# One pass of 512 columns for the high weights in the MLP's down projections, modulation rows and attention bias spread over the MLP, first softmax groups normalised by GpSimd

## The chip, the core and the metric

One core of a Trainium2 chip runs the whole program as one launch. The metric is the time of an execution in device microseconds (us). Two of the executions of the kernel before are within 0.1% of each other, and the third is 0.5% above them.

## What is computed

The program takes 256 tokens of width 1024 through three layers: a recurrent layer with an MLP, a sparse attention layer with an MLP, and a hybrid layer of neighbourhood attention and two convolution branches. The change touches the MLPs, the softmax of the attention layer, and the modulation rows of the third layer:

```python
def sq_relu_mlp(h, w_up, w_down):
    return jnp.square(jax.nn.relu(h @ w_up)) @ w_down

    for layer in range(DEPTH):
        ...
        x = x + mix
        x = x + sq_relu_mlp(rms_norm(x, norm_mlp_g[layer]), mlp_w_up[layer], mlp_w_down[layer])

    # attention layer, per block of 128 queries
        p = jax.nn.softmax(logits, axis=-1).astype(c.dtype)

def modulate(x, cond, norm_g, w_ada, b_ada):
    shift, scale, gate = jnp.split(jax.nn.silu(cond) @ w_ada + b_ada, 3, axis=-1)
    ...
    return rms_norm_2(x, norm_g) * (1 + scale) + shift, gate
```

`w_up` is 1024 x 4096 and `w_down` 4096 x 1024. `modulate` is taken of the tokens with `c_2` and of the context with `c_ctx_2`; the gate rows are wanted for the tokens alone.

## The kernel before

Activations lie transposed: a tile is 128 features by 256 tokens. Every matrix is cut into chunks of 128 x 1024 numbers (512 KB), eight 128 x 128 blocks each. 266 chunks pass through a ring of four slots: SyncE's queue loads `raw`, ScalarE copies it to the reduced type (`whi`, the high part), VectorE subtracts (`wlo`, the low part), and TensorE multiplies. SyncE loads the next chunk into a slot as soon as VectorE has made `wlo` of the old one. The activations are split in the same way. The function `acc3` makes one product tile from three passes into one accumulator: high weights by high activations (L546), high weights by low activations (L550), low weights by high activations (L551). Each pass loads its 128 x 128 weights and streams 256 columns.

An MLP has two stages. In the first (`up0`, `up1`: 16 units of two chunks) VectorE takes the relu, ScalarE squares it twice into `hhi` and `sqb`, and VectorE makes `hlo`. In the second (`down0`, `down1`: 16 units) two units, that is four chunks or 32 blocks, make one output tile m of eight: 96 passes into the first 256 columns of bank 0 or 1, in turn. VectorE adds the bank to `x[:, m]` (L1696), ScalarE makes `xh` of it, VectorE `xl`, and the next stage (`lat` after `down0`, the context's keys `ck` after `down1`) multiplies by these; it can begin with its tiles k = 0 to 6 and needs k = 7 last. Between the first and the second half of `down0` a full-precision product with `ones` (L598) sums the context's squares. In the unit after it the table PACE cuts six of the first passes in two (L548, L549). The same table is used in one unit each of `up0`, `up1` and `gates`.

The modulation needs 24 row tiles of `w_ada`, 512 KB each, loaded by GpSimd's queue into two slots (`load_ada`), each reduced against `cond` by VectorE: twice for shift and scale tiles, once for the 8 gate tiles. Eight tiles (two reduces each) lie beside `up0` (`ada_beside`, L1631), sixteen (24 reduces) beside `down0` (`ada_tile`, L1558), two per m. The loads of the attention bias `relB`, 8 of 256 KB, are issued one per m in `down0` behind GpSimd's addition of squares.

The attention layer's softmax runs in 12 groups. Per group TensorE makes logits (L799, L804), VectorE adds the bias and takes the maximum (`read_logits`, L1803), ScalarE takes the exponential and its sums, VectorE inverts the sums and scales `pt` (`norm_probs`, L1813), TensorE transposes (L813) and multiplies by V (L825). Groups 0 to 3 have four pieces of 128 x 128, the others two of 128 x 256. The last four of the eight rounds of the top-k search and the scaling of the last queries (`queries(3)`, L1773) stand between these groups on VectorE. TensorE's logits of group 3 wait for `queries(3)`.

The order on each engine is the order of the code, written out by hand. `quads` is a loop over groups of four units.

## Time and profile before

| | us |
|---|---|
| three executions | 861.98, 862.42, 866.18 |
| median | 862.42 |
| profiled execution | 861.54 |
| its span, first to last instruction | 859.5 |

| stage | us from the span's start |
|---|---|
| recurrent layer | 0 to 94 |
| `up0`, `down0` | 94 to 184, 184 to 273 |
| `lat`, `q`, search, attention, `att_out` | 273 to 380 |
| `up1`, `down1` | 380 to 468, 468 to 555 |
| third layer | 555 to 859 |

In the rows, PE is TensorE's matmul stream, PEld its weight loads, DVE VectorE, ACT ScalarE, POOL GpSimd, SPq SyncE's queue. A row of the time order has the start, the duration, the engine, the line, the operation, what it writes and reads, the shape and the number of instructions merged, and in brackets the idle time before it and what ended it. A matmul's duration is its passage through the array and overlaps its neighbours': what it costs is the distance from its start to the next one's.

### The profile page before, as it was taken

How to read it: one execution, taken by the hardware profiler on the slowest of the kernel's cores; microseconds unless marked ns; L12 is line 12 of the kernel's file. 1: busy time of each engine (PE TensorE's matmuls, PEld its weight loads, DVE VectorE, ACT ScalarE, POOL GpSimd, SP SyncE). 2: the span in 40 equal slices, each digit the busy share in tenths (PEclk: the TensorE clock that was granted, in tenths of full speed). 3: DMA queues.
4: the chain of work that ended last, by engine and by line, in shares of the span. 5: the costliest groups of instructions: out<-in, count | busy, mean ns of one | idle time of the engine just before them, and what ended most of it. 6: DMA issues, size and time to landing. Idle time of an engine off the chain costs nothing.

```text
span 859.5 us, 18107 instructions
## 1 busy us (share of the span) xinstructions
PE 848.9 (99%) x7062; PEld 813.6 (95%) x7062; DVE 698.2 (81%) x1096; ACT 484.3 (56%) x710; POOL 130.0 (15%) x147
## 2 busy tenths in 40 slices
PE   8999999999999999999999999999999999999998
PEld 7999999999999997799999999989899898999998
DVE  5998798898888899786667666677758998998895
ACT  6796555555444466765555444363367557645742
POOL 3140000014322000000000222132203314012000
PEclk9999999999999999999999999999999999999999
DMA  8744667779999730246666666576445554455552
GB/s 318 299 149 147 221 229 245 244 258 294 296 289 267 216 128 20 93 162 214 196 195 196 203 193 195 167 214 220 149 148 172 171 161 159 148 174 177 207 180 98
DMA packets 48050, 167.88 MB, mean 195 GB/s; under 512 B 5969, under 2 KB 7393, under 8 KB 47729
## 3 DMA queue, kind: packets, MB, share of 16 engines
q1 hardware_dynamic: 41840, 146.82, 52.0%
q0 software_dynamic: 5856, 20.00, 8.0%
q8 instruction: 47, 0.77, 0.4%
q14 instruction: 19, 0.15, 0.1%
q10 hardware_dynamic: 288, 0.15, 0.1%
HBM read 165.50 MB, written 1.44 MB: 194 GB/s over the span
## 4 chain that ended last, share of the span: by engine, by line
PE 74%; DVE 14%; DMA 6%; ACT 3%; issue 2%; SPq 0%; POOL 0%; DVEq 0%; ACTq 0%
PE bank L546 22%; PE bank L550 22%; PE bank L551 22%; DMA raw<-weights 5%; DVE wlo L1416 4%; DVE xc L1498 1%; DVE ada_prod L1558 1%; PE bank L813 1%; ACT whi L1030 1%; PE bank L898 1%; PE bank L900 1%; PE bank L899 1%; PE bank L939 1%; PE bank L949 1%; DMA x<-x_in 1%
## 5 line engine op out<-in xcount | busy, mean ns | idle before, releaser
L1416 DVE TENSOR_TENSOR wlo<-raw,whi 128x1024 fp32r<-128x1024 f32 x266 | 326.8, 1262 | 86.1 <-ACT whi L1030 85.5
L550 PE MATMUL bank<-xl,whi 128*128 128x256 f32 x1328 | 369.7, 278 | 0.0
L546 PE MATMUL bank<-xh,whi 128*128 128x256 f32 x1310 | 367.5, 281 | 1.9 <-DVE xl L1438 1.7
L551 PE MATMUL bank<-xh,wlo 128*128 128x256 f32 x1328 | 368.4, 277 | 0.0
L1030 ACT ACTIVATE whi<-raw 128x1024 fp32r<-128x1024 f32 x266 | 272.3, 1054 | 152.6 <-PE bank L551 99.6
L546 PEld LDWEIGHTS bank<-xh,whi 128*128 128x128 f32 x1310 | 245.8, 188 | 10.9 <-issue 7.1
L550 PEld LDWEIGHTS bank<-xl,whi 128*128 128x128 f32 x1328 | 249.4, 188 | 0.3
L551 PEld LDWEIGHTS bank<-xh,wlo 128*128 128x128 f32 x1328 | 249.2, 188 | 0.0
L551 PE MATMUL bank<-hhi,wlo 128*128 128x256 f32 x560 | 155.1, 277 | 0.0
L546 PE MATMUL bank<-hhi,whi 128*128 128x256 f32 x554 | 154.1, 278 | 0.0
L550 PE MATMUL bank<-hlo,whi 128*128 128x256 f32 x512 | 142.2, 278 | 0.0
L551 PEld LDWEIGHTS bank<-hhi,wlo 128*128 128x128 f32 x560 | 105.2, 188 | 0.0
L546 PEld LDWEIGHTS bank<-hhi,whi 128*128 128x128 f32 x554 | 104.0, 188 | 0.3
L550 PEld LDWEIGHTS bank<-hlo,whi 128*128 128x128 f32 x512 | 96.1, 188 | 0.0
L1175 ACT ACTIVATE hhi<-tq 128x512 f32 (+1 forms) x32 | 20.3, 635 | 73.2 <-DVE tq L1665 73.2
L1965 DVE SCALAR_TENSOR_TENSOR cu<-up,cols,cu 128x256 f32<-128x256 f32 x120 | 49.1, 480 | 0.0
L412 POOL TENSOR_TENSOR acc<-acc,sqt 128x256 f32<-128x256 f32 x16 | 18.7, 1169 | 183.6 <-ACT sqt L1192 183.6
L546 PE MATMUL bank<-hch,whi 128*128 128x256 f32 x160 | 45.6, 285 | 0.4 <-DVE hcl L1821 0.4
L550 PE MATMUL bank<-hcl,whi 128*128 128x256 f32 x160 | 44.6, 279 | 0.0
L551 PE MATMUL bank<-hch,wlo 128*128 128x256 f32 x160 | 44.6, 279 | 0.0
L546 PEld LDWEIGHTS bank<-hch,whi 128*128 128x128 f32 x160 | 30.0, 188 | 1.5 <-issue 0.7
L1558 DVE CUSTOM_DVE_ANT_0 ada_prod<-ada_raw,cond 128x1024 f32<-128x1024 f32 x24 | 29.9, 1245 | 1.4
(311 smaller groups left out, 1032.1 us busy)
## 6 DMA issues: line engine op xcount, KB each, us to landing
raw<-weights SPq DMA_DIRECT2D x266, 512.0 KB, 4.3
ada_raw<-ada_w POOLq DMA_DIRECT2D x24, 512.0 KB, 5.7
plain<-plain_w SPq DMA_DIRECT2D x8, 512.0 KB, 8.5
relB<-rel_scratch POOLq DMA_DIRECT2D x8, 256.0 KB, 8.8
bl<-rpb_in POOLq DMA_DIRECT2D x32, 64.0 KB, 3.4
plain<-plain_w SPq DMA_DIRECT2D x4, 256.0 KB, 5.7
cond<-cond_in POOLq DMA_DIRECT2D x1, 1024.0 KB, 8.5
cx<-ctx_in POOLq DMA_DIRECT2D x1, 1024.0 KB, 8.5
```

The source lines that it names most:

```text
L412: ins = G.tensor_tensor(acc[:, 0], acc[:, 0], sqt[:, 0], ALU.add)
L546: mmul(dst, hi, rh, start=start, stop=False)
L550: mmul(dst, hi, rlo, start=False, stop=False)
L551: return mmul(dst, lo, rh, start=False, stop=stop)
L813: mm = nc.tensor.transpose(TURN[:, i * P:(i + 1) * P], src[:, g % depth, i * P:(i + 1) * P], ident[:])
L898: mmul(dst, rh[:, k, tok], wh, start=k == 0, stop=False)
L899: mmul(dst, rh[:, k, tok], wl, start=False, stop=False)
L1030: A(whi[:, sl], raw[:, sl], ACT.Copy).then_inc(S_["w_hi_ready"], 1)
L1175: A(hhi[:, bass.ds(q * 8 + 2 * (r - u0), 2)], tq[:, r % 2], ACT.Square).then_inc(S_["h_hi"], 1)
L1416: V_.tensor_tensor(wlo[:, sl], raw[:, sl], whi[:, sl].bitcast(F32), ALU.subtract)\
L1558: ins = V_.tensor_tensor_reduce(ada_prod[:], ada_raw[:, slot], cond[:, c], 1.0, 0.0, ALU.mult, ALU.add, dst(c))
L1965: ins = V_.scalar_tensor_tensor(cu[:, t], up[:, t, k:k + S], wk, cu[:, t], ALU.mult, ALU.add)
```

## The change

- In both down stages the block of high weights is multiplied by the high and the low activations in one pass of 512 columns (`h2` holds `hhi` and `hlo` in one tensor); the results lie in the two halves of the bank. The low weights' pass goes into the first half. VectorE adds both halves to `x[:, m]`, one after the other. The cut passes of `down0` go.
- Of the 24 row tiles two gate tiles (one reduce each) go to the stage before `up0`, eight stay in `up0`, fourteen (22 reduces) are left in `down0`, three reduces per m at most and two in m = 4 and m = 7. The order of the tiles is changed to suit.
- All eight `relB` loads are issued in `up0`, one behind each row load.
- `norm_probs` of groups 0 to 3 is done by GpSimd after VectorE has inverted the sums.
- The first plain weights are loaded by halves of a chunk (2 KB per partition in one piece), where it was quarters of two chunks, and their first slot is freed earlier.

```diff
-ADA_ORDER = [0, 1, 2, 3, 4, 5, 6, 7, 8, 16, 9, 17, 10, 18, 11, 19, 12, 20, 13, 21, 14, 22, 15, 23]
+ADA_ORDER = [16, 17, 0, 1, 2, 3, 4, 5, 6, 7, 8, 18, 9, 19, 10, 20, 11, 21, 12, 13, 22, 14, 23, 15]
-ADA_DOWN = 8
+ADA_UP = 2
+ADA_DOWN = ((10, 11), (12, 13), (14, 15), (16, 17), (18,), (19, 20), (21, 22), (23,))
...
-            hhi = sb("hhi", [P, FT, S], F32R, room)
-            hlo = sb("hlo", [P, FT, S], F32R, room)
+            h2 = sb("h2", [P, 2, FT, S], F32R, room)
+            hhi, hlo = h2[:, 0], h2[:, 1]
...
-                sp.dma_start(plain[:, 0:2, part], plain_w[0:2, :, part].rearrange("c p n -> p c n")).then_inc(s_head[j], 16)
+                sp.dma_start(plain[:, j // 2, part], plain_w[j // 2][:, part]).then_inc(s_head[j], 16)
...
+            load_ada(2)
+            load_ada(3)
             pool.wait_ge(S_["chunk_used"], 2 * U0["up0"])
             pool.dma_start(cx[:], ctx_in).then_inc(S_["ctx_loaded"], 16)
-            for i in range(2, ADA_DOWN + 2):
-                load_ada(i)
...
+            pool.wait_ge(S_["rel_stored"], 16)
+            for m in range(DT):
+                load_ada(4 + m)
+                load_rel_bias(m)
             pool.dma_start(wiw[:], wi_in).then_inc(S_["wi_loaded"], 16)
-            pool.wait_ge(S_["rel_stored"], 16)
-            squares_by_tile(3, 0, ahead_of_tile, load_rel_bias)
+            squares_by_tile(3, 0, ahead_of_tile)
...
+            for g in range(4):
+                pool.wait_ge(S_["sums_inverted"], g + 1)
+                for i in range(4):
+                    sl = slice(i * P, (i + 1) * P)
+                    ins = G.tensor_scalar(pt[:, g % 3, sl], pt[:, g % 3, sl], rden[:, g % 2, i:i + 1], None, ALU.mult)
+                ins.then_inc(S_["probs_ready"], 1)
...
-                            mm = acc3(b[:, 0:S], (2 * r + c) % 4, k * P, hhi[:, kt], hlo[:, kt], kt == 0, kt == FT - 1,
-                                      pace.get((c, k)))
+                            sl, w = (2 * r + c) % 4, slice(k * P, (k + 1) * P)
+                            mmul(two(b), whi[:, sl, w], h2[:, :, kt], start=kt == 0, stop=False)
+                            mm = mmul(b[:, 0:S], wlo[:, sl, w], hhi[:, kt], start=False, stop=kt == FT - 1)
...
-                    quads(pe, u0 + 8, u0 + 9, lambda q, r: unit(q, r, PACE))
-                    quads(pe, u0 + 9, u0 + NUNITS["down0"], unit)
+                    quads(pe, u0 + 8, u0 + NUNITS["down0"], unit)
...
                 add_pair(0, j)
+                if j in (1, 2):
+                    ada_tile(j - 1)
...
-                        ada_tile(ADA_DOWN + 2 * m)
-                        ada_tile(ADA_DOWN + 2 * m + 1)
+                        for i in ADA_DOWN[m]:
+                            ada_tile(i)
...
-                    emptied(V_.tensor_tensor(x[:, m], bank[(F0["down" + name] + m) % 2][:, 0:S], x[:, m], ALU.add))
+                    b = bank[(F0["down" + name] + m) % 2]
+                    ch.link(V_.tensor_tensor(x[:, m], b[:, 0:S], x[:, m], ALU.add))
+                    emptied(V_.tensor_tensor(x[:, m], b[:, S:2 * S], x[:, m], ALU.add))
...
-                ch.link(V_.reciprocal(rden[:, g % 2, 0:2 * nt], den[:, g % 2, 0:2 * nt]))
+                ins = V_.reciprocal(rden[:, g % 2, 0:2 * nt], den[:, g % 2, 0:2 * nt])
+                if g < 4:
+                    ins.then_inc(S_["sums_inverted"], 1)
+                    return
+                ch.link(ins)
+                if g == 4:
+                    dve.wait_ge(S_["probs_ready"], 4)
```

TensorE in the middle of `down0`, at the product with `ones`, before the change. L546 and L550 read the same block of `whi`:

```order
L546 MATMUL bank<-hhi,whi 128x256
L550 MATMUL bank<-hlo,whi 128x256
L551 MATMUL bank<-hhi,wlo 128x256
L598 MATMUL bank<-R,ones 128x256
L546 MATMUL bank<-hhi,whi 128x256
L550 MATMUL bank<-hlo,whi 128x256
L551 MATMUL bank<-hhi,wlo 128x256
L548 MATMUL bank<-hhi,whi 128x128
L549 MATMUL bank<-hhi,whi 128x128
L550 MATMUL bank<-hlo,whi 128x256
```

The same place in the changed kernel, where `h` is the tensor `h2`, L715 the wide pass, L716 the pass of the low weights and L607 the product with `ones`:

```order
L715 MATMUL bank<-h,whi 128x512
L716 MATMUL bank<-h,wlo 128x256
L607 MATMUL bank<-R,ones 128x256
L715 MATMUL bank<-h,whi 128x512
L716 MATMUL bank<-h,wlo 128x256
L715 MATMUL bank<-h,whi 128x512
L716 MATMUL bank<-h,wlo 128x256
```

Three passes of 256 columns have become one of 512 and one of 256, and the cut passes are gone.

VectorE at the last tile, m = 7, of `down0`, before. L1558 is a reduce of a row tile, L1696 the addition to x, L1438 the low part that `lat` waits for:

```order
L1438 SCALAR_TENSOR_TENSOR xl<-x,cols,xh 128x256
L1558 ISA ada_prod,ada<-ada_raw,cond 128x1024
L1558 ISA ada 128x1
L1558 ISA ada_prod,ada<-ada_raw,cond 128x1024
L1558 ISA ada 128x1
L1558 ISA ada_prod,ada<-ada_raw,cond 128x1024
L1558 ISA ada 128x1
L1416 TENSOR_TENSOR wlo<-raw,whi 128x1024
L1696 TENSOR_TENSOR x<-bank,x 128x256
L1438 SCALAR_TENSOR_TENSOR xl<-x,cols,xh 128x256
```

The same place in the changed kernel (L1568 the reduce, L1708 and L1709 the additions, L1448 the low part):

```order
L1448 SCALAR_TENSOR_TENSOR xl<-x,cols,xh 128x256
L1568 ISA ada_prod,ada<-ada_raw,cond 128x1024
L1568 ISA ada 128x1
L1568 ISA ada_prod,ada<-ada_raw,cond 128x1024
L1568 ISA ada 128x1
L1426 TENSOR_TENSOR wlo<-raw,whi 128x1024
L1708 TENSOR_TENSOR x<-bank,x 128x256
L1709 TENSOR_TENSOR x<-bank,x 128x256
L1448 SCALAR_TENSOR_TENSOR xl<-x,cols,xh 128x256
```

Two reduces stand where three stood, and one addition more.

GpSimd from the last context-independent work before `up0` on, before (L438 squares the decay, L389 a row load, L441 the context, L448 a `relB` load):

```order
L438 TENSOR_TENSOR a<-ra 128x512 x2
L441 DMA cx<-ctx_in 128x2048
L389 DMA ada_raw<-ada_w 128x1024 x8
L468 DMA wiw<-wi_in 128x64
L393 MEMSET acc 128x512
L459 TENSOR_TENSOR R<-R,sqt 128x256
L389 DMA ada_raw<-ada_w 128x1024 x2
L412 TENSOR_TENSOR acc<-acc,sqt 128x256
L448 DMA relB<-rel_scratch 16x16x256
```

And in the changed kernel (L390 a row load, L444 the context, L449 a `relB` load):

```order
L439 TENSOR_TENSOR a<-ra 128x512 x2
L390 DMA ada_raw<-ada_w 128x1024 x2
L444 DMA cx<-ctx_in 128x2048
L390 DMA ada_raw<-ada_w 128x1024
L449 DMA relB<-rel_scratch 16x16x256
L390 DMA ada_raw<-ada_w 128x1024
L449 DMA relB<-rel_scratch 16x16x256
```

Two row loads have moved ahead of the context, and the `relB` loads stand among the row loads of `up0`.

## Rows read from the trace of the kernel before

**Rows 1.** The page: busy time, share of the span and instructions by engine.
```profile
PE 848.9 (99%) x7062; PEld 813.6 (95%) x7062; DVE 698.2 (81%) x1096; ACT 484.3 (56%) x710; POOL 130.0 (15%) x147
```

**Rows 2.** Busy us (count) by engine, PEclk, DMA share, GB/s: `up0`, `down0`, `down1`.
```profile
94.00:184.00 90.00, 90.00 (x791) 89.95 (x791) 79.58 (x105) 52.37 (x69) 4.30 (x8) 1.00 0.72 240
184.00:276.00 92.00, 91.41 (x787) 90.95 (x785) 79.29 (x102) 40.70 (x56) 28.06 (x38) 1.00 0.97 289
...
469.00:555.00 86.00, 86.00 (x761) 86.00 (x761) 57.55 (x68) 37.96 (x47) 16.52 (x14) 1.00 0.64 200
```

**Rows 3.** Time order of TensorE in `down1`: two starts, nine passes apart.
```profile
469.17 0.28 PE L546 MATMUL bank<-hhi,whi 128*128 128x256 f32 x1
...
470.19 0.28 PE L546 MATMUL bank<-hhi,whi 128*128 128x256 f32 x1
```

**Rows 4.** The same in `down0`: a cut triple; then two starts nine passes apart.
```profile
227.76 0.25 PE L548 MATMUL bank<-hhi,whi 128*128 128x192 f32 x1
...
228.21 0.28 PE L546 MATMUL bank<-hhi,whi 128*128 128x256 f32 x1
...
232.32 0.28 PE L546 MATMUL bank<-hhi,whi 128*128 128x256 f32 x1
...
233.38 0.28 PE L546 MATMUL bank<-hhi,whi 128*128 128x256 f32 x1
```

**Rows 5.** The same in the context's values: two starts, 47 wide passes apart.
```profile
567.01 0.39 PE L898 MATMUL bank<-whi,hch 128*128 128x512 f32 x1
...
577.97 0.39 PE L900 MATMUL bank<-whi,hcl 128*128 128x512 f32 x1
```

**Rows 6.** Time order of TensorE where `down0` ends and `lat` waits.
```profile
272.66 0.28 PE L551 MATMUL bank<-hhi,wlo 128*128 128x256 f32 x1
...
275.13 0.28 PE L551 MATMUL bank<-xh,wlo 128*128 128x256 f32 x1
277.15 0.39 PE L546 MATMUL bank<-xh,whi 128*128 128x256 f32 x1 [1.75 <-DVE xl L1438]
```

**Rows 7.** Time order of VectorE at the same place.
```profile
267.46 1.23 DVE L1416 TENSOR_TENSOR wlo<-raw,whi 128x1024 fp32r<-128x1024 f32 x1 [1.87 <-ACT whi L1030]
...
275.62 0.42 DVE L1696 TENSOR_TENSOR x<-bank,x 128x256 f32<-128x256 f32 x1
```

**Rows 8.** Groups of VectorE within `down0` (count | busy us, mean ns | idle before).
```profile
L1416 DVE TENSOR_TENSOR wlo<-raw,whi 128x1024 fp32r<-128x1024 f32 x31 | 39.1, 1279 | 11.2 <-ACT whi L1030 11.2
L1558 DVE CUSTOM_DVE_ANT_0 ada_prod<-ada_raw,cond 128x1024 f32<-128x1024 f32 x24 | 29.9, 1245 | 1.4
```

**Rows 9.** Who waited for whom within `down0`: us in total, times, longest.
```profile
ACT whi L1030 <- DMA raw<-weights: 38.4, 18, 3.8
```

**Rows 10.** Time order of VectorE in the stage ahead of `up0`.
```profile
94.27 0.69 DVE L1473 TENSOR_TENSOR x<-bank,x 128x512 f32<-128x512 f32 x1 [1.30 <-PE bank L551]
```

**Rows 11.** Time order of VectorE in the attention layer's first groups.
```profile
325.71 0.88 DVE L1813 TENSOR_SCALAR pt<-pt,rden 128x128 f32<-128x128 f32 x4
...
331.28 0.69 DVE L1773 SCALAR_TENSOR_TENSOR qT<-bank,R 128x512 f32<-128x512 f32 x1
```

**Rows 12.** Time order of TensorE at the same place.
```profile
330.07 0.60 PE L813 MATMUL bank<-ident,pt 128*128 128x128 f32 x4
332.03 0.50 PE L799 MATMUL bank<-amask,identr 128*128 128x256 f32 x2 [1.36 <-DVE qT L1773]
...
337.93 0.66 PE L813 MATMUL bank<-ident,pt 128*128 128x128 f32 x4
```

**Rows 13.** Groups of GpSimd over the whole span.
```profile
L412 POOL TENSOR_TENSOR acc<-acc,sqt 128x256 f32<-128x256 f32 x16 | 18.7, 1169 | 183.6 <-ACT sqt L1192 183.6
...
L479 POOL TENSOR_TENSOR cx<-cx,rctx 128x256 f32<-128x256 f32 x8 | 7.7, 960 | 0.1
...
L380 POOL MEMSET ones<- 128x128 f32 x1 | 0.2, 205 | 0.3 <-POOLq L2227 0.3
```

**Rows 14.** Time order of VectorE at the end of `down1`.
```profile
555.04 0.42 DVE L1696 TENSOR_TENSOR x<-bank,x 128x256 f32<-128x256 f32 x1 [3.12 <-PE bank L551]
```

35 lines of the change are left out of this document (18 added, 17 removed).

## The prediction

> **What bounds the kernel now.** I read the page first: TensorE is busy for 99% of the span [rows 1]. Since passes overlap in the array, busy time says little about speed, so I went to the windows by stage and then to the time order, for the distance from one start to the next. In `up0`, `down0` and `down1` TensorE's stream has no hole worth the name, and the granted clock is 1.00, the 2.4 GHz level [rows 2]. A pass of 256 columns would take 0.1067 us at that clock. It takes more, and not always the same: in `down1` nine passes start within 1.02 us, 0.1133 each; in the second half of `down0` nine take 1.06 us, 0.1178 each [rows 3, 4]. Between these no engine is waited for, so TensorE has two paces, and it keeps one until something breaks the stream. `down0` is in the faster pace until the product with `ones`, and in the slower after it. Second, in `down0` the DMA engines are full (share 0.97 against 0.72 and 0.64 in the MLP stages around it [rows 2]), and ScalarE waited 38.4 us in 18 pieces for raw weights [rows 9]. TensorE does not stall on that inside the stage; it pays once, at the end, where `lat` waits for the last tile of x [rows 6]. Third, at the first softmax groups VectorE is what TensorE waits for [rows 12].
>
> **The change part by part.**
>
> *The wide pass.* Each down stage has 256 blocks, today three passes each: in `down0` 128 blocks at 3 x 0.1133 = 0.340 us and 128 at 3 x 0.1178 = 0.3534, in `down1` 256 at 0.340; together 43.5 + 45.2 + 87.0 = 175.8 us. The columns that are streamed stay 768 per block; what can be saved is what a pass costs beside its columns. Call the new time of a block T; the sum is 512 T. Three values:
> - If the 0.0067 us that a pass takes beyond its columns is a fixed cost, the wide pass takes 0.2133 + 0.0067 = 0.2200 and T = 0.3333.
> - The only wide passes of this kind in the trace are those of the context's values: 47 passes from 567.01 to 577.97 us, 0.233 each [rows 5]. That is 0.020 beyond the columns, more than twice the fast 256-column pass (0.2267) and less than twice the slow one (0.2356). So the excess goes with the columns, not with the instruction. With a fast pass of the low weights T = 0.233 + 0.1133 = 0.3463.
> - Both paces carried over: T = 0.340 all fast, 0.3534 all slow.
> The nearest row says 0.346, but there one wide pass follows another, while here each is followed by a narrow one, as the stream that today runs at 0.340 is all narrow. I take the middle of 0.340 and 0.347, 0.3437 rounded to 0.344: 176.1 us, **+0.3**. The ends are 170.6 (-5.2) and 181.0 (+5.2).
>
> The trace's wide pass takes 0.233 us. The Trainium skill (TensorE: Matmul & The Clock Gate, section Back-to-back issue gap) gives N/2.4 + 2.5 ns, 216 ns for 512 columns, as the gap of an isolated warm pass; the trace disagrees by 17 ns, and by the rule T would be 0.216 + 0.113 = 0.329. It is a rival below, since nothing in the rows says why these passes are slower.
>
> *The cut passes of `down0`.* A cut triple takes 228.21 - 227.76 = 0.45 us where an uncut one takes 0.353 [rows 4]; six of them, **-0.6**. They did not bring the fast pace back here, so nothing is lost with them that the trace has.
>
> *The end of `down0`.* The last pass of `down0` starts at 272.66, the stream goes on with `lat` to 275.13 and stands until 277.15 [rows 6]: a hole of 2.02, less one pass, 1.9 us. VectorE adds the last bank at 275.62 [rows 7], 3.0 us after the last pass; in `down1` the same addition starts at 555.04, as soon as TensorE is done [rows 14]. VectorE is late because from 267.46 it has split two chunks, made `xl`, done three reduces and split a third chunk, and because the first of these waited 1.87 us for ScalarE, which had waited for the DMA. The change takes one reduce of 1.25 us [rows 8] from this m and relieves the DMA: in `down0` there are two row loads of 0.52 MB and eight bias loads of 0.26 MB less, 3.1 of about 26.5 MB, so the share falls to some 0.86. It adds an addition, 0.42 and a wait of 0.04. With VectorE on time, the last low part is ready about 0.3 (end of the product) + 1.53 (today from 275.62 to 277.15) + 0.46 = 2.3 us after the last pass of the stage starts, and the 21 passes of `lat` that lie ahead take 2.5. So the hole closes, without room to spare. If only the reduce counts, 1.25 - 0.46 = 0.8 is gained. I take **-1.7**, with -0.8 and -1.9 as ends.
>
> VectorE's own work per m is four splits (5.1), at most three reduces (3.7 and their read-outs 0.25), `xl` (0.5) and two additions (0.9): 10.5 us against 32 T = 11.0. It fits. Were T at 0.33, it would be level, and VectorE would be what is late next.
>
> *Rows in the stage ahead of `up0`.* One reduce of 1.25 + 0.08 us goes into each of two idle stretches of VectorE like the one of 1.30 before 94.27 [rows 10]. **+0.1** for what sticks out; the ends are 0 and 0.3.
>
> *Bias loads in `up0`.* 2.1 MB go into 90 us, 23 GB/s on 240 at a share of 0.72 [rows 2]; the share rises to 0.8. Nothing on GpSimd waits behind them but the next row load, and the bias is read 100 us later. **0**. The head's loads carry the same bytes in the same order: **0**, with 0.3 either way.
>
> *GpSimd's normalisation.* VectorE loses 4 x 0.88 us [rows 11]. Two of the four stand ahead of `queries(3)`, which today starts at 331.28 and lets TensorE go on at 332.03 after 1.36 us of idling [rows 12]. The queries' own product ends where the transposition starts, at 330.07, and its results are there some 0.3 later, so VectorE can gain 0.9 of the 1.7 us there. What is next late is GpSimd: the chain is inverse, four scalings, transposition. Let p be one scaling. By my estimate from the order of the work group 2's sums will be inverted at 333.5 and group 3's at 335.5, and the groups follow each other on GpSimd, so group 3 is ready at the latest of 325.7 + 16 p, 333.5 + 8 p and 335.5 + 4 p; it is wanted today at 337.93 and, if all comes 0.5 earlier, at 337.4. The break-even is p = 0.5 us. The trace has no such operation on GpSimd. From below there is a MEMSET of the same shape, 0.205; from above a product of two tensors of twice the columns, 0.960 with VectorE calm and 1.169 otherwise [rows 13]. A scaling reads one tensor and lies nearer to the MEMSET; I take 0.35: **-0.5**. The ends are -0.9 (p = 0.2) and +3.3 (p = 0.96).
>
> *The end of `down1`.* The addition of 0.46 us starts the chain of VectorE that ends in `ctx_lo` of the last tile [rows 14], for which TensorE waits in `ck` already today: **+0.45**.
>
> The sum is 0.3 - 0.6 - 1.7 + 0.1 - 0.5 + 0.45 = -1.95, so the profiled execution of 861.54 (span 859.5) would become 859.6. The executions shown lie 0.4 and 0.9 above the profiled one, the third far above; with 0.6 for that I predict **860.2 us**. A measurement of this kernel tells 0.5%, 4.3 us, from no change.
>
> **The rivals.**
>
> *A pass has a fixed cost, T = 0.333.* For it: 256 passes fewer in each stage, each with a weight load fewer, and PEld is as busy as PE there [rows 2]. Against it: the wide passes of the trace. 512 x 0.0107 = 5.5 less: 854.7.
>
> *The wide pass at 216 ns, T = 0.329.* The mechanism is the same, with the whole excess gone from the wide pass: 512 x 0.0147 = 7.5 less, 852.7; a little of it would go to VectorE, which needs 10.5 us per m. This is the skill's formula quoted above; rows 5 speak against it.
>
> *The slow pace throughout, T = 0.3534.* Each wide pass breaks the stream as the product with `ones` does today, and `down1`, now fast, falls to 0.3534 as well. 4.8 more: 865.0, still within 0.5%.
>
> *GpSimd is too slow, and slower than before is the outcome.* With p = 1.17, the row of the additions that run beside a busy VectorE [rows 13], group 3 is ready at 325.7 + 18.7 = 344.4 instead of 337.9, and everything behind it moves by 6.5 us; the 0.5 gained is gone as well: 867.2, 0.6% slower. It decides from p = 1.1 on. For it: VectorE works without a pause there, and GpSimd's operations of one shape vary with what VectorE does. Against it: half the columns, one tensor read.
>
> *The DMA is no better.* If the bytes taken out of `down0` do not shorten the raw loads, 1.1 us of the hole stays: 861.1. It is inside the forecast's own range.
>
> **How the numbers follow.** Forecast, T from 0.340 to 0.349, 860.2 with its own range 857.8 to 863.5: 0.50, of which 0.07 is more than 0.5% faster than before. Fixed cost: 0.20. T = 0.329: 0.08. Slow pace: 0.14, of which 0.03 beyond +0.5% together with a dear GpSimd. GpSimd alone: 0.08. Faster is 0.07 + 0.20 + 0.08 = 0.35, slower 0.03 + 0.08 = 0.11, the same 0.54. The range runs from 853.5, just below the fixed-cost case, to 866.0; it leaves out the formula's case and GpSimd's.
>
> **What would show it.** In the time order of TensorE in `down1`, the distance from one wide pass to the next is T: 0.344 here, 0.333 and 0.353 for the rivals. After the product with `ones` no cut passes follow; whether the pace changes there is open. Where `lat` begins, the hole before its last tile should be under 0.3 us, with the DMA share of `down0` near 0.86 and ScalarE's wait for raw weights well below 38 us. One scaling of `pt` on GpSimd should take 0.25 to 0.5 us, and the transposition that starts at 337.93 should come 0.5 earlier against `queries(3)`'s product. The prediction is wrong if T lies outside 0.340 to 0.349, or if the other stages, which run at either pace (0.1133 or 0.1178) by what broke their stream, change theirs: 10 us of passes at the other pace are worth 0.4 us.

## The result and the profile after

The changed kernel takes 866.97 us (median of 12 executions, 865.38 to 873.22) where the kernel before takes 861.12 (12 executions, 859.35 to 866.18). The ratio is 1.0078, 95% interval 1.0058 to 1.0099 (the two medians alone give 1.0068): **slower by 0.8%**, where 860.2 was forecast and 866.0 was the upper end. The profiled execution took 866.93 with a span of 864.7, against 861.54 and 859.5.

The page, busy time by engine, as in [rows 1], and under it the windows of `up0`, `down0` and `down1`, as in [rows 2]:

```profile
PE 856.2 (99%) x6544; PEld 796.9 (92%) x6544; DVE 698.6 (81%) x1096; ACT 484.8 (56%) x710; POOL 137.5 (16%) x163
```

```profile
94.00:184.00 90.00, 90.00 (x788) 89.77 (x787) 78.75 (x106) 52.31 (x68) 8.87 (x16) 1.00 0.89 262
184.00:276.00 92.00, 91.86 (x525) 79.77 (x524) 79.06 (x108) 42.62 (x59) 23.23 (x30) 1.00 0.82 272
469.00:559.00 90.00, 90.00 (x512) 78.48 (x511) 61.57 (x77) 38.22 (x47) 16.51 (x14) 1.00 0.60 191
```

TensorE has 518 matmuls fewer and is busy for 7 us longer. The last two numbers of a window are the DMA's busy share and GB/s. The DMA has moved from `down0` (0.97 to 0.82) to `up0`, and there the share went from 0.72 to 0.89 for a rate that rose from 240 to 262 GB/s only.

To find where 5.3 us of span went I set the start of the same pass in both traces side by side; the difference is how far the changed kernel lags. Four passes of the changed kernel, in time order of TensorE: the product with `ones`, the first pass of the last tile in `lat` [rows 6], a pass near the start of `down1` (the first of [rows 3]) and the last pass of all:

```profile
228.41 0.59 PE L607 MATMUL bank<-R,ones 128*128 128x256 f32 x2
...
276.55 0.28 PE L555 MATMUL bank<-xh,whi 128*128 128x256 f32 x1
...
470.40 0.40 PE L715 MATMUL bank<-h,whi 128*128 128x512 f32 x1
...
860.93 0.28 PE L560 MATMUL bank<-hch,wlo 128*128 128x256 f32 x1
```

They start at 226.15, 277.15, 469.17 and 855.67 in the kernel before. At the second of them the lag is -0.60; from the next pass on it is -0.72, since in the kernel before the pass behind the hole takes 0.23 us and not 0.12. By stage:

| stage | forecast, us | measured, us | lag after it |
|---|---|---|---|
| up to the start of `down0` | +0.1 | 0.0 | 0.0 |
| first half of `down0` | +0.5 (pace) | +2.25 (1.7 pace, 0.6 waits) | 2.26 |
| cut passes gone | -0.6 | -0.68 | 1.58 |
| second half of `down0` | -1.2 (pace) | -0.28 (a wait gone) | 1.30 |
| end of `down0` | -1.7 | -2.02 | -0.72 |
| attention's first groups | -0.5 | +1.94 | 1.22 |
| `down1` | +1.0 (pace) | +3.38 | 4.60 |
| end of `down1` | +0.45 | +0.44 | 5.04 |
| third layer | 0 | +0.22 | 5.26 |
| sum | -1.95 | +5.26 | |

**The pace.** TensorE in `down1`, two wide passes, twelve blocks apart:

```profile
479.94 0.40 PE L715 MATMUL bank<-h,whi 128*128 128x512 f32 x1
...
484.18 0.40 PE L715 MATMUL bank<-h,whi 128*128 128x512 f32 x1
```

4.24 / 12 = 0.3533 us per block, three passes at the slow pace of 0.1178 us of [rows 4]. The sum is the same in both down stages, its parts are not: on the average a wide pass takes 0.230 and the narrow one behind it 0.123 in `down1`, 0.239 and 0.114 in the second half of `down0`.

**A wait for weights**, in the time order of TensorE early in `down0`. From 196.60 to the next start there are 0.42 us instead of 0.12. The row loads and `relB` loads come closest together here: GpSimd issues row loads at 181.4, 188.3, 193.4 and 196.1, where they were some 10 us apart in `up0`, and `relB` loads at 181.9 and 188.8:

```profile
196.60 0.28 PE L716 MATMUL bank<-h,wlo 128*128 128x256 f32 x1
197.02 0.51 PE L715 MATMUL bank<-h,whi 128*128 128x512 f32 x1
```

**The end of `down0`.** VectorE at the last tile [rows 7], and who waited for whom within the stage [rows 9]. VectorE now stands idle for 2.22 us before the first addition, where it was 3 us late, and ScalarE waits 13.9 us for raw weights in place of 38.4:

```profile
274.27 0.42 DVE L1708 TENSOR_TENSOR x<-bank,x 128x256 f32<-128x256 f32 x1 [2.22 <-PE bank L716]
```

```profile
ACT whi L1040 <- DMA raw<-weights: 13.9, 8, 4.7
```

**GpSimd and the clock.** GpSimd's scalings, then TensorE in the same place (compare [rows 12]), then windows of two us: TensorE's busy time (count), granted clock, DMA share, GB/s:

```profile
325.07 2.36 POOL L487 TENSOR_SCALAR pt<-pt,rden 128x128 f32<-128x128 f32 x4 [40.12 <-DVE rden L1823]
...
332.99 4.75 POOL L487 TENSOR_SCALAR pt<-pt,rden 128x128 f32<-128x128 f32 x8 [2.70 <-DVE rden L1823]
```

```profile
330.37 0.50 PE L809 MATMUL bank<-amask,identr 128*128 128x256 f32 x2 [0.42 <-DVE qT L1786]
...
335.39 0.65 PE L823 MATMUL bank<-ident,pt 128*128 128x128 f32 x4 [1.63 <-POOL pt L487]
...
338.24 1.11 PE L823 MATMUL bank<-ident,pt 128*128 128x128 f32 x4
339.29 1.10 PE L835 MATMUL bank<-pT,V 128*64 128x128 f32 x8
```

```profile
334.00:336.00 2.00, 0.61 (x6) 1.00 0.00 0
336.00:338.00 2.00, 2.00 (x15) 0.71 0.00 0
338.00:340.00 2.00, 2.00 (x14) 0.50 0.00 0
```

TensorE waits 0.42 us for `queries(3)` where it waited 1.36, as forecast. But a scaling takes 0.59 us, so the four of group 2 end at 335.35, and TensorE waits 1.63 us for them. Behind that wait the granted clock falls to 0.50, the 1.2 GHz level, and the work from 338.24 to 340.32 takes 2.08 us; the same work took 1.18 from 337.93 in the kernel before. GpSimd itself had finished group 3 at 337.74.

### The profile page after: what moved, and what is told of

Read it like the earlier page. It is cut to its first block, busy times and chain, and to the rows that moved or that the text cites. A ratio compares the mean times of both kernels' runs of the same rounds, so it can differ in the third digit from the quotient of the medians.

```text
span 864.7 us, 17109 instructions
## 1 busy us (share of the span) xinstructions
PE 856.2 (99%) x6544; PEld 796.9 (92%) x6544; DVE 698.6 (81%) x1096; ACT 484.8 (56%) x710; POOL 137.5 (16%) x163
## 4 chain that ended last, share of the span: by engine, by line
PE 87%; DVE 4%; DMA 3%; ACT 3%; issue 1%; POOL 0%; SPq 0%; DVEq 0%; ACTq 0%
PE bank L555 19%; PE bank L559 18%; PE bank L560 18%; PE bank L715 13%; PE bank L716 7%; DMA raw<-weights 2%; PE bank L823 2%; PE bank L650 1%; DVE wlo L1426 1%; PE bank L949 1%; PE bank L959 1%; PE bank L908 1%; PE bank L910 1%; PE bank L909 1%; ACT whi L1040 1%
## 5 line engine op out<-in xcount | busy, mean ns | idle before, releaser
L715 PE MATMUL bank<-h,whi 128*128 128x512 f32 x512 | 181.5, 396 | 0.1
L716 PE MATMUL bank<-h,wlo 128*128 128x256 f32 x512 | 144.3, 282 | 0.0
L715 PEld LDWEIGHTS bank<-h,whi 128*128 128x128 f32 x512 | 96.2, 188 | 23.8 <-DVE wlo L1426 0.9
L716 PEld LDWEIGHTS bank<-h,wlo 128*128 128x128 f32 x512 | 96.1, 188 | 0.0
L1185 ACT ACTIVATE h<-tq 128x512 f32 (+1 forms) x32 | 20.3, 634 | 71.8 <-DVE tq L1676 71.8
L390 POOL DMA_DIRECT2D ada_raw<-ada_w x24 | 13.1, 546 | 146.6 <-DVE ada L1644 84.9
L1059 ACT ACTIVATE xh<-x,cols 128x256 fp32r<-128x256 f32 x32 | 14.6, 503 | 36.3 <-DVE x L1709 19.4
L1568 DVE CUSTOM_DVE_ANT_0 ada_prod<-ada_raw,cond 128x1024 f32<-128x1024 f32 x24 | 29.7, 1239 | 2.6 <-DMA ada_raw<-ada_w 1.5
```

Source lines behind the costliest of these rows:

```text
L715: mmul(two(b), whi[:, sl, w], h2[:, :, kt], start=kt == 0, stop=False)
L716: mm = mmul(b[:, 0:S], wlo[:, sl, w], hhi[:, kt], start=False, stop=kt == FT - 1)
L1185: A(hhi[:, bass.ds(q * 8 + 2 * (r - u0), 2)], tq[:, r % 2], ACT.Square).then_inc(S_["h_hi"], 1)
L1568: ins = V_.tensor_tensor_reduce(ada_prod[:], ada_raw[:, slot], cond[:, c], 1.0, 0.0, ALU.mult, ALU.add, dst(c))
```

## The experiments

Each ran on one chip beside the kernel before; ratios are to it, of timed executions. "Lag" is the distance between the starts of the same pass in two traces, as above.

### The two suspects undone, one at a time and together

**a1**: VectorE normalises all groups again; the rest of the change stays.

```diff
-                ins = V_.reciprocal(rden[:, g % 2, 0:2 * nt], den[:, g % 2, 0:2 * nt])
-                if g < 4:
-                    ins.then_inc(S_["sums_inverted"], 1)
-                    return
-                ch.link(ins)
+                ch.link(V_.reciprocal(rden[:, g % 2, 0:2 * nt], den[:, g % 2, 0:2 * nt]))
...
-            for g in range(4):
-                pool.wait_ge(S_["sums_inverted"], g + 1)
...
```

> The changed kernel with one part undone: VectorE normalises softmax groups 0 to 3 again; the wide pass, the spread of rows and bias and the head loads stay. Theory (two separate losses, the pace of the down stages and the attention layer): the changed kernel's TensorE is 0.6 us ahead of the kernel before where the attention layer starts (332 us) and 1.2 us behind it at 340 us, so 1.8 us come back: span 864.7 - 1.8 = 862.9, the granted clock 1.00 in all of 330 to 345 us, the transposition of group 3 within 0.7 us of 337.3, and a median some 2 us under the changed kernel's 866.97. Rival: the clock falls because of the wide passes' load, not because TensorE waits for GpSimd; then the granted clock still falls near 336 to 342 us and less than 1 us comes back.

Measured: 865.21 us, ratio 1.0038 (1.0022 to 1.0054), span 863.0, clock 1.000. TensorE of a1, group 3's transposition, and its clock:

```profile
337.44 0.66 PE L817 MATMUL bank<-ident,pt 128*128 128x128 f32 x4
```

```profile
336.00:338.00 2.00, 1.91 (x16) 1.00 0.00 0
338.00:340.00 2.00, 2.00 (x18) 1.00 0.00 0
```

The theory's 862.9 was met, and the wide passes were still there: what is lost in the attention layer is lost by GpSimd's part. Between the two traces it is 1.9 us by the lag; the spans differ by 1.7, since a1 waits longer for weights at 197 us (0.8 us, the changed kernel 0.3).

**a2**: three passes of 256 columns and the cut passes are back, GpSimd's part stays.

```diff
-                            sl, w = (2 * r + c) % 4, slice(k * P, (k + 1) * P)
-                            mmul(two(b), whi[:, sl, w], h2[:, :, kt], start=kt == 0, stop=False)
-                            mm = mmul(b[:, 0:S], wlo[:, sl, w], hhi[:, kt], start=False, stop=kt == FT - 1)
+                            mm = acc3(b[:, 0:S], (2 * r + c) % 4, k * P, hhi[:, kt], hlo[:, kt], kt == 0, kt == FT - 1,
+                                      pace.get((c, k)))
...
-                    ch.link(V_.tensor_tensor(x[:, m], b[:, 0:S], x[:, m], ALU.add))
-                    emptied(V_.tensor_tensor(x[:, m], b[:, S:2 * S], x[:, m], ALU.add))
+                    emptied(V_.tensor_tensor(x[:, m], bank[(F0["down" + name] + m) % 2][:, 0:S], x[:, m], ALU.add))
```

> The changed kernel with another part undone: three passes of 256 columns per block in the down stages, one addition per tile and the cut passes in down0, as before; GpSimd's normalisation, the spread of rows and bias and the head loads stay. Theory: the wide pass costs 13 ns per block wherever the stream ran at 0.340 us per block: 3.4 us in down1 and 0.5 at its end, and in down0 about 1.0; 4.9 us less, span near 859.8, blocks at 0.340 us in down1 and in the first half of down0, 0.353 in the second half of down0. Rival: the hole of 1.9 us at the end of down0 closed only because the slower blocks gave VectorE and the DMA more time; then a hole of 1 to 1.9 us is back before the last tile of lat and the span is 861 or more. The clock falls near 336 us as in the changed kernel by the theory.

Measured: 861.48 us, ratio 0.9991 (0.9973 to 1.0009), span 862.1, clock 0.998. The pace came back as expected (`down1` gives 3.4 us), the second half of `down0` is at 0.340 as well, which was not expected, and the hole at its end stays closed, against the rival. But the span is 2.3 us over the forecast, for a reason that I had not in any theory. The profiled execution is also one of the slow ones: it took 864.24, the others 858.7 to 865.1. TensorE of a2 at the start of `down0`, and the windows there:

```profile
195.33 0.28 PE L560 MATMUL bank<-h,wlo 128*128 128x256 f32 x1
199.34 0.39 PE L555 MATMUL bank<-h,whi 128*128 128x256 f32 x1 [3.73 <-DVE wlo L1426]
```

```profile
196.00:198.00 2.00, 0.00 (x0) 1.00 0.95 209
198.00:200.00 2.00, 0.66 (x5) 1.00 1.00 400
200.00:202.00 2.00, 2.00 (x13) 0.58 1.01 387
```

The raw weights came late: the DMA is full (0.95 to 1.01), TensorE stood for 4.0 us, and then ran at the low clock for some 3 us. The changed kernel waits at the same place, for 0.3 us. So the `relB` loads in `up0`, priced at 0, are a third suspect.

**a3**: both undone, with the edits of a1 and a2 together; the spread of rows and bias and the head loads are left.

> Both parts undone: three passes of 256 columns with the cut passes, VectorE normalises all groups; what is left of the change is the spread of rows and bias loads and the head loads. Theory: the sum of the two others, 864.7 - 1.8 - 4.9 = 858.0, which is 1.5 us under the span of the kernel before (859.5), by the hole at the end of down0, with a clock of 1.000; a ratio to the kernel before of 0.998. Rival (hole closed only by the slower blocks): span 859.3 to 860, ratio 1.000.

Measured: 860.23 us, ratio 0.9985 (0.9969 to 1.0001), span 858.5, clock 1.000. The hole at the end of `down0` is closed (2.1 us gained). But `up0` is slower. TensorE of a3 in `up0`, one pass of each block, twelve blocks apart, before and behind a small break:

```profile
135.81 0.28 PE L549 MATMUL bank<-xh,whi 128*128 128x256 f32 x1
...
139.90 0.28 PE L549 MATMUL bank<-xh,whi 128*128 128x256 f32 x1
...
141.14 0.28 PE L554 MATMUL bank<-xh,wlo 128*128 128x256 f32 x1
141.37 0.39 PE L549 MATMUL bank<-xh,whi 128*128 128x256 f32 x1
...
141.83 0.28 PE L549 MATMUL bank<-xh,whi 128*128 128x256 f32 x1
...
146.07 0.28 PE L549 MATMUL bank<-xh,whi 128*128 128x256 f32 x1
```

4.09 / 12 = 0.341 us before, 4.24 / 12 = 0.353 behind it. The break is 0.2 us long, and what follows it is 13 ns more in each block up to the product with `ones`: the lag to the kernel before grows from -0.2 at 145.69 to +2.8 at 219.58 us. In return the cut passes, which there meet no wait, bring 0.340 back for the second half of `down0` (-1.5 us), which they fail to do in the kernel before.

**a4**: GpSimd normalises groups 0 and 1 only.

```diff
-            for g in range(4):
+            for g in range(2):
...
-                if g < 4:
+                if g < 2:
...
-                if g == 4:
-                    dve.wait_ge(S_["probs_ready"], 4)
+                if g == 2:
+                    dve.wait_ge(S_["probs_ready"], 2)
```

> The changed kernel with GpSimd normalising only groups 0 and 1; VectorE normalises groups 2 and 3. Theory: the two scalings groups ahead of queries(3) on VectorE stay taken off it, so TensorE goes on at queries(3) 0.9 us earlier than in a1 (which undoes all four groups), and nothing waits for GpSimd's 2.36 us per group at 335 us: span 0.5 to 0.9 us under a1's, clock 1.00 in 330 to 345 us. Rival: VectorE's two groups behind queries(3) then end as late as they would anyway and set the transposition of group 3, so the 0.9 us is lost again and the span is that of a1 within 0.2; or GpSimd's group 1 (ready 2 x 2.36 us after the first sums) is itself late and the clock still falls.

Measured: 863.47 us, ratio 1.0025 (1.0005 to 1.0044), span 860.9, clock 1.000. From a1 to a4 the lag changes by -0.64 up to 197 us (0.45 of it a shorter wait for weights, chance) and by -0.94 at `queries(3)`, the 0.9 expected; no wait for GpSimd is left. The spans differ by 2.1, where 0.5 to 0.9 was expected: besides the 0.64, another 0.5 comes in the third layer, and what brought it is not shown.

### Does the width of the pass set the pace?

**c1**: the same products, halves and additions, but two passes of 256 columns in place of the one of 512.

```diff
-                            mmul(two(b), whi[:, sl, w], h2[:, :, kt], start=kt == 0, stop=False)
+                            mmul(b[:, 0:S], whi[:, sl, w], hhi[:, kt], start=kt == 0, stop=False)
+                            mmul(b[:, S:2 * S], whi[:, sl, w], hlo[:, kt], start=False, stop=False)
```

> The changed kernel, but the pass of 512 columns is two passes of 256 (hhi into the first half of the bank, hlo into the second), with the same weights and the same two additions on VectorE. Theory (the instruction's width sets the pace): down1 runs at 0.340 us per block, 3.4 us less than the changed kernel's there. Rival (two halves of the bank, or the state in which the stage is entered, set it): 0.353 us per block stays in down1.

Measured: one execution, 861.93 us, span 859.7. `down1`, twelve blocks apart:

```profile
479.90 0.28 PE L715 MATMUL bank<-h,whi 128*128 128x256 f32 x1
...
483.98 0.28 PE L715 MATMUL bank<-h,whi 128*128 128x256 f32 x1
```

4.08 / 12 = 0.340. With the same two halves of the bank and the same additions, the width makes the difference: over `down1` it is worth 3.4 us, and `down0` too begins at 0.340 here, where the changed kernel is at 0.3533 from its start. But narrow passes alone do not keep the fast pace. Behind a wait of 0.4 us at 219 us c1 is slow, and as it has no cut passes it stays slow behind the product with `ones`, to the end of `down0`:

```profile
240.18 0.28 PE L715 MATMUL bank<-h,whi 128*128 128x256 f32 x1
...
244.42 0.28 PE L715 MATMUL bank<-h,whi 128*128 128x256 f32 x1
```

4.24 / 12 = 0.353. In this execution the clock stayed at 1.00 behind the same wait of 1.63 us for GpSimd, and in the attention's first groups it gains 1.3 us on the changed kernel: what the low clock cost there.

**c2**: passes of the low weights cut in two, in one unit of `down0` and in three of `down1`.

```diff
+                            f = pace.get((c, k))
+                            if f is not None:
+                                mmul(b[:, 0:f], wlo[:, sl, w], hhi[:, kt, 0:f], start=False, stop=False)
+                                mm = mmul(b[:, f:S], wlo[:, sl, w], hhi[:, kt, f:S], start=False, stop=kt == FT - 1)
```

> The changed kernel with some passes of the low weights cut in two (six at 128 or 192 columns in the first unit of the second half of down0, and in down1 in units 4, 8 and 12: six at 128 or 192, four at 64, six at 128 or 192 in a row). Theory (the stream of wide and narrow passes has paces too, and a stall at the right place brings the fast one): behind one of these units the distance from one wide pass to the next is 0.340 or 0.349 us instead of 0.3533 (the changed kernel shows 0.349 from 208 to 219 us, behind a wait), down to the end of the stage. Rival (a wide pass fixes the slow pace): 0.353 us after each of them, and the span is longer by what the cuts cost, 22 passes more at some 0.1 us, 1 to 2 us.

Measured: one execution, 868.39 us, span 866.3. The first three units leave 0.3533 as it was, the fourth brings 0.349 for the last 20 us of `down1`:

```profile
544.71 0.39 PE L715 MATMUL bank<-h,whi 128*128 128x512 f32 x1
...
548.90 0.39 PE L715 MATMUL bank<-h,whi 128*128 128x512 f32 x1
```

4.19 / 12 = 0.349. By the lag the cuts cost some 2 us in all (0.6 in `down0`, 1.5 in `down1`), and the last gave 0.2 back. No run shows a wide stream at 0.340; that none exists is not shown.

### Where the relB loads can go

All of these have three passes with the cut passes, GpSimd for groups 0 and 1, and the row tiles spread as in the change.

**b2**: the eight `relB` loads back in `down0`.

```diff
             for m in range(DT):
                 load_ada(4 + m)
-                load_rel_bias(m)
...
-            squares_by_tile(3, 0, ahead_of_tile)
+            squares_by_tile(3, 0, ahead_of_tile, load_rel_bias)
```

> Three passes of 256 columns with the cut passes in down0, GpSimd normalises groups 0 and 1 only, row tiles spread as in the changed kernel, but the eight relB loads go back to down0, one per m. Theory: the relB loads fill the DMA in up0 (share 0.94 to 1.02 there in the changed kernel, 0.72 before), which makes TensorE wait for weights (0.23 us at 141 us in a3, 0.4 us at 196.6 us in the changed kernel, 4.0 us at 195.3 us in a2), and such a wait can change the pace from 0.340 to 0.353 us per block for what follows. With them in down0: DMA share of up0 back at 0.70 to 0.80, no distance above 0.15 us between passes from 106 to 225 us, 0.340 us per block there; in down0 the DMA is full again, short waits come behind the product with ones, the pace there stays at 0.353, and the hole before the last tile of lat is 0.5 to 1.9 us. Span 857.0 to 858.5. Rival: the row tiles alone fill the DMA of up0 (then the share stays above 0.9 and the waits stay), or the hole was closed by the rows alone (then it is under 0.3 us here).

Measured: 859.24 us, ratio 0.9969 (0.9949 to 0.9989), span 857.6. Windows of `up0` and `down0`, and TensorE behind the product with `ones`:

```profile
94.00:184.00 90.00, 90.00 (x792) 89.95 (x792) 79.68 (x107) 51.91 (x69) 4.76 (x9) 1.00 0.72 248
184.00:276.00 92.00, 91.28 (x789) 91.02 (x788) 78.08 (x100) 42.95 (x60) 27.01 (x37) 1.00 0.96 284
```

```profile
230.06 0.28 PE L559 MATMUL bank<-h,wlo 128*128 128x256 f32 x1
231.06 0.39 PE L554 MATMUL bank<-h,whi 128*128 128x256 f32 x1 [0.72 <-DVE wlo L1425]
```

`up0` is at 0.72 and keeps 0.340. In a3, with the loads in `up0`, the share there was 0.90: by that the eight loads take 0.18 x 90 = 16 us of a full DMA. From the share of `down0`, 0.96 here and 0.82 in a3, it is 13. By their 2.1 MB at the rate of `up0` before (240 GB/s at 0.72, 333 at a full DMA) it would be 6.3. The 1.0 us wait falls among the cut passes, and the second half of `down0` stays at the slow pace. The hole before the last tile of `lat` is closed, where 0.5 to 1.9 us were expected; the rows alone can have done it, or the wait and the slow pace ahead of it.

**b3**: the eight loads behind `lat`, from 277 us on.

```diff
             G.tensor_tensor(csq[:], ci[:, 0], ci[:, 0], ALU.mult).then_inc(S_["c_square"], 1)
+            pool.wait_ge(S_["rel_stored"], 16)
+            for m in range(DT):
+                load_rel_bias(m)
```

> As b2, but the eight relB loads are issued behind lat (from about 277 us), where the kernel before has a DMA share of 0.3 to 0.65; they are read from about 318 us. Theory: up0 keeps 0.340 us per block as in b2; down0 has 4.2 MB of transfers less than before and a DMA share under 0.9, the cut passes bring 0.340 back for the second half of down0 (128 blocks at 13 ns less, 1.7 us), and the hole before the last tile of lat is under 0.3 us (1.9 us less); queries(3) lets TensorE go on 0.9 us earlier as in a4. Span 859.5 - 1.7 - 1.9 - 0.9 = 855.0, with 0.2 less by the head, ratio to the kernel before 0.995. Rivals: the relB loads delay the raw weights of q (a wait of TensorE between 280 and 320 us) or come too late for the first softmax group (VectorE waits at 318 us), then 1 to 3 us are given back; or the cut passes do not work here either, then 856.7.

Measured: 865.26 us, ratio 1.0029 (1.0008 to 1.0049), span 864.3, clock 0.995. In `down0` all that was expected came: lag to b2 -1.95 at 271 us. Then the rival came, larger than I had it. Windows of b3, and TensorE at the end of the queries:

```profile
290.00:300.00 10.00, 10.00 (x89) 1.00 1.03 170
300.00:310.00 10.00, 8.69 (x74) 1.00 1.04 169
318.00:322.00 4.00, 4.00 (x20) 0.50 0.76 259
```

```profile
314.15 0.28 PE L561 MATMUL bank<-xh,wlo 128*128 128x256 f32 x1
317.65 0.55 PE L556 MATMUL bank<-cnh,whi 128*128 128x256 f32 x1 [3.22 <-DVE wlo L1427]
```

A full DMA (1.03), with raw weights and `relB` together, moves 170 GB/s here, where a2's full DMA moved 387 at 200 us: the `relB` loads cost time that their bytes do not tell. GpSimd's queue moved 2.29 MB from 270 to 320 us and took 29.7% of the 16 engines for it, 15 us. A load writes 16 partitions in 16 pieces of 1 KB each; the profile counts it in packets of more than 2 KB. The Trainium skill (DMA: Bandwidth & Descriptors, section Specifications) has pieces from 512 bytes on at the full rate; these runs do not bear that out for this load. Which of its traits makes it slow, the pieces, the few partitions or the source rows, each of which starts 4 bytes off the last, no run here shows.

**b4**: every second `relB` load in `up0`, the others in `down0`.

```diff
             for m in range(DT):
                 load_ada(4 + m)
-                load_rel_bias(m)
+                if m % 2 == 0:
+                    load_rel_bias(m)
...
-            squares_by_tile(3, 0, ahead_of_tile)
+            squares_by_tile(3, 0, ahead_of_tile, lambda m: load_rel_bias(m + 1) if m % 2 == 0 else None)
```

> As b2 (three passes, cut passes, GpSimd for groups 0 and 1, rows spread), with relB loads 0, 2, 4, 6 in up0 behind every second row load and 1, 3, 5, 7 in down0 behind tiles m = 0, 2, 4, 6. All eight cost 15 us of a full DMA (share of the 90 us of up0 0.72 without, 0.89 with them). Theory: half of them in each stage gives shares near 0.80 in up0 and 0.89 in down0, TensorE waits for no weights in either, up0 and the first half of down0 stay at 0.340 us per block, the cut passes bring 0.340 for the second half of down0: the 1.0 us wait of b2 at 230 us and 128 x 13 ns go: span 857.6 - 2.7 = 854.9, ratio to the kernel before 0.994. Rival: what matters is not the share over the stage but two transfers that fall together; then a wait of 0.2 us or more stays in one of the stages, the pace falls there and the span is 856 to 858.

Measured: 856.94 us (856.19 to 857.23), ratio 0.9936 (0.9912 to 0.9961), span 855.2. **It is faster than both kernels**, 0.6% against the kernel before, where b2 was 0.3%. Its four executions lie within 1.0 us; the 25 of the kernel before beside it spread over 5.5. Windows, and TensorE in the second half of `down0`, twelve blocks apart:

```profile
94.00:184.00 90.00, 90.00 (x792) 89.94 (x791) 79.50 (x106) 52.12 (x68) 7.08 (x13) 1.00 0.81 257
184.00:276.00 92.00, 92.00 (x811) 91.95 (x810) 79.78 (x107) 44.25 (x61) 26.11 (x35) 1.00 0.91 282
```

```profile
253.86 0.28 PE L556 MATMUL bank<-h,whi 128*128 128x256 f32 x1
...
257.94 0.28 PE L556 MATMUL bank<-h,whi 128*128 128x256 f32 x1
```

0.340 per block, and between 107 and 276 us TensorE waits for no weights. The expected 854.9 was met. Its lead on the kernel before is 1.2 us at 272 us, 3.5 behind the hole, 4.4 behind `queries(3)`, 4.3 at the end.

**b5**: as b4, with the second four behind `lat`.

```diff
             G.tensor_tensor(csq[:], ci[:, 0], ci[:, 0], ALU.mult).then_inc(S_["c_square"], 1)
+            for m in range(1, DT, 2):
+                load_rel_bias(m)
```

> As b4, but the four relB loads 1, 3, 5, 7 are issued together behind lat (277 us), where all eight held the raw weights back by up to 9 us in b3. Theory: four of them fill the DMA for 7 to 8 us from 277 us on; four raw slots cover some 6 to 8 us, so TensorE waits 0 to 1 us near 307 us; down0 as in b3 (0.340 us per block in its second half, no wait at 230 us, share 0.76). Span 855.0 to 856.5. Rival: the wait near 307 us is 1.5 us or more and breaks the pace of what follows or the clock, then 857 or more.

Measured: 863.42 us, ratio 1.0017 (1.0004 to 1.003), span 862.8. The rival again: two waits of TensorE, 1.6 and 1.7 us (starts at 310.05 and 317.61), and one of 0.5 at 196.3. The granted clock stayed at 1.00 behind all of them. Loads that are issued together hold the next raw chunks back, four as well as eight.

### One part of the change alone, in the kernel before

**d1**: the `relB` loads alone go to `up0`.

```diff
+            pool.wait_ge(S_["rel_stored"], 16)
             for i in range(2, ADA_DOWN + 2):
                 load_ada(i)
+                load_rel_bias(i - 2)
             pool.dma_start(wiw[:], wi_in).then_inc(S_["wi_loaded"], 16)
-            pool.wait_ge(S_["rel_stored"], 16)
-            squares_by_tile(3, 0, ahead_of_tile, load_rel_bias)
+            squares_by_tile(3, 0, ahead_of_tile)
```

> The kernel before with one thing of the change alone: the eight relB loads stand in up0, one behind each row load, and none in down0. Theory: the DMA share of up0 goes from 0.72 to about 0.89 and that of down0 from 0.97 to about 0.81; TensorE waits for weights once or twice between 130 and 200 us, 0.2 to 4 us, by which the pace of some of up0 or down0 falls from 0.340 to 0.353 us per block; the end of down0 gains (part of the hole of 1.9 us). The sum is open in sign: span 857.5 to 863, with a wider spread of its runs than the kernel before has. Rival (bytes alone count): share 0.80 in up0, no wait, span 857.5 to 858.5.

Measured: 860.04 us, ratio 0.9991 (0.9965 to 1.0017); its ten executions are spread from 857.74 to 866.36. The profiled one is the fastest of them and met no wait: span 855.8, share 0.85 in `up0` and 0.84 in `down0`, hole closed, fast pace in all of `down0`. That is all of b4's gain in `down0` without a row moved. By the spread of the times not every execution has it; the slower ones were not profiled. The share of 0.85 lies between the rival's 0.80 and the theory's 0.89.

**d2**: the wide pass alone, in both down stages, with its second addition and without the cut passes.

```diff
-                            mm = acc3(b[:, 0:S], (2 * r + c) % 4, k * P, hhi[:, kt], hlo[:, kt], kt == 0, kt == FT - 1,
-                                      pace.get((c, k)))
+                            sl, w = (2 * r + c) % 4, slice(k * P, (k + 1) * P)
+                            mmul(two(b), whi[:, sl, w], h2[:, :, kt], start=kt == 0, stop=False)
+                            mm = mmul(b[:, 0:S], wlo[:, sl, w], hhi[:, kt], start=False, stop=kt == FT - 1)
```

> The kernel before with the wide pass alone (in both down stages, with the second addition and without the cut passes); rows, bias, head and normalisation as before. Theory: 0.353 us per block everywhere in down0 and down1: +1.7 in the first half of down0, -0.6 for the cut passes, +3.4 in down1, +0.5 at its end, and the hole at the end of down0 is shorter by what the slower first half gives the DMA and by nothing else, 0 to 1 us: span 859.5 + 4.0 to 5.0 = 863.5 to 864.5, ratio 1.005. Rival (hole closed by the slower blocks): the hole is gone, span 862.6.

Measured: 864.74 us, ratio 1.0052 (1.0029 to 1.0075), span 862.5. TensorE where the hole was:

```profile
276.33 0.38 PE L546 MATMUL bank<-xh,whi 128*128 128x256 f32 x1 [0.55 <-DVE xl L1438]
```

1.75 us of idling have become 0.55: 1.2 us are gained with no transfer and no reduce moved. The rival was nearer than the theory. How the wide passes do it is not shown: `down0` takes only 0.4 us longer than in the kernel before, and ScalarE waits as long for raw weights (38.9 us, 38.4 before), but VectorE waits less for ScalarE (7.0 us, 11.2 before). Another 0.4 us came from the pace, 0.349 in place of 0.3533 from 243 us on, behind a break of 0.1 us.

## Why the prediction was wrong

**The wide pass (forecast +0.3, measured +5.1 for 512 T).** The term failed at one choice. The prediction weighed the wide passes of [rows 5], found that the excess goes with the columns, and then took the narrow pass behind a wide one at the fast pace (0.1133) or better, 0.344 in all. The wide pass takes the 0.233 us of the row only on the average of both stages. In the second half of `down0` the narrow pass is nearly as fast as was assumed (0.114), but there the wide one takes 0.239; in `down1` it is 0.230 and 0.123. What holds is the sum, 0.3533. That 0.233 is also twice 0.1166, near the slow pace, was seen, and the reading was left to a rival: *the slow pace throughout*, T = 0.3534, chance 0.14. It was the case that came. Of its mechanism c1 confirms that the width brings the slow pace in `down1` and at the start of `down0`; "each wide pass breaks the stream" is not shown. The Trainium skill's formula for the gap of an isolated pass (TensorE: Matmul & The Clock Gate, Back-to-back issue gap), 216 ns at 512 columns, is not met by any run here; the shortest average over a stretch was 229 ns, in the changed kernel from 209 to 217 us.

**GpSimd (forecast -0.5, measured +1.9).** Three things were wrong. The first is the price p: 0.35 taken, 0.59 measured. The two rows that were to bound it were 0.205 (a MEMSET) and 0.96, and I went to the lower one because a scaling reads one tensor. With p = 0.59 the prediction's own chain gives 333.5 + 8p = 338.2 for group 3, 0.3 later than before, so the term would have been +0.3; the break-even was put at 0.5. That group 3 was indeed transposed at 338.24 is luck: GpSimd was done at 337.74, and TensorE came late by its low clock (337.46 in c1, where the clock stayed at 1.00). The second is group 2, whose own limit I did not work out: TensorE waits for it first. The third is the clock, which was not in the sum at all: 1.3 of the 1.9 us. The gain at `queries(3)` was 0.93, forecast 0.9.

The clock does not fall each time. It was below 0.999 in 9 of 12 executions of the changed kernel and in 6 of 10 of a2, where the wait of 4.0 us can have done it too; in a1, a3 and a4 in 4 of 29, and in the kernel before beside them in 6 of 30. The changed kernel's executions with the clock at 1.000 took 865.4 to 865.9 us, the others 866.7 to 873.2. One fall costs 1.3 us, so it does not explain the whole spread, and d2 had one execution of 871.15 at 1.000. What decides within one kernel whether the clock falls is open: a2's profile has the same wait of 1.61 us at 337.95 and keeps 1.00 behind it; c1 does too, and so does b5 behind waits of 1.6 and 1.7 us for weights.

**Bias loads in `up0` (forecast 0, measured +0.6 in the profiled execution).** The step "the share rises to 0.8" was made from bytes, and the loads take two to two and a half times what their bytes say; it rose to 0.89. Where they fall close to the row loads at the start of `down0`, TensorE waits, 0.3 us in the changed kernel, 4.0 in a2, not at all in d1's profile; with the loads back in `down0` (b2) there is no wait there.

**The end of `down0` (forecast -1.7, measured -2.0).** Right in size, and there is no wait at 276.55. "Without room to spare" was wrong: VectorE has 2.2 us of it. The causes given are not separated by the result: bias out (d1), rows out (b2, beside a 1 us wait of TensorE) and wide passes (d2, 1.2 of it) each closed most of it alone.

**The cut passes (-0.6, measured -0.7).** Right for this kernel. "They did not bring the fast pace back here, so nothing is lost" was short-sighted: in a2, a3, b3, b4, b5 and d1, where no wait falls among them, they do bring it back, worth 1.5 us. In the kernel before one pass among them comes late (0.22 us from 229.78 on), in b2 there is the wait of 1.0 us, and there they fail. The change took the cut passes away; whether they would have helped beside wide ones is doubtful after c2.

**The end of `down1` (+0.45, measured +0.44), rows ahead of `up0` (+0.1, measured 0.0).** Right.

The two large misses were each near a rival of the prediction, though GpSimd cost its 2.4 us at a price far below that rival's p = 1.1, by the clock. They came together, to which only 0.03 was given: 865.0 of the slow pace plus 2.4 for GpSimd is 867.4, and the median is 867.0. The range was drawn from single cases and ended at 866.0. That the sum comes out so close is partly luck, since the smaller terms cancel.

## What to carry to other kernels

- Before merging instructions to save their fixed cost, look whether the stream shows more than one pace. If it does, price the new stream at the slow one too, and check what the old stream did to keep the fast one. Here the slow pace came and not the average.
- A wait of 0.2 us in a stream that runs at a fast pace can cost ten times its length (3 us in a3), and the cut passes restored the pace only where no wait fell among them. So a transfer that is "hidden" must be spread: price it by the DMA's busy share in a stretch where it runs, and issue it one piece at a time.
- Handing work from a busy engine to an idle one is bounded by the idle one's time per piece. Work out the limit for every group in the chain, not for the last alone, and leave room: in the changed kernel's profile a wait of TensorE of 1.6 us cost 1.3 us more in granted clock.

## What the runs showed that was not expected

- TensorE's passes of 256 columns run at 0.1133 or 0.1178 us, and a stream with wide ones at 0.3533 or 0.3490 us per 768 columns. Behind a break of 0.2 us it went from the fast to the slow pace (a3), behind one of 0.1 us at 208 us it did not (c1), behind the six cut passes it was fast again (a2, a3, b3, b4, b5, d1), without them it stayed slow (c1), and with wide passes the fast pace of 0.340 was never seen. Why there are two is open.
- After TensorE had stood for 4.0 us (a2), 3.5 (b3) or, sometimes, 1.6 us (the changed kernel), the granted clock fell to 0.50 for some three us (a2) to six (b3), although TensorE was busy again. Behind waits of 1.6 and 1.7 us it also stayed at 1.00 (a2, b5, c1).
- Eight loads of 256 KB, to 16 partitions each in pieces of 1 KB, took 13 to 16 us of the whole DMA, where their bytes at the rate of `up0` would take 6.3; while they ran beside the raw weights, a full DMA moved 170 GB/s, and 387 without them.
- A scaling of 128 x 128 on GpSimd takes 0.59 us, against 0.22 on VectorE (0.88 for four, [rows 11]).
